# Eight split slots in the raw slots' memory, stage seams by tile and column half, high and low parts from PSUM

## What is computed

```python
shift, scale, gate = _modulation(c, ada_w[i], ada_b[i])      # silu(c) @ ada_w: 1024 x 3072 weights per layer
hx = _rmsnorm(x, norm_g[i]) * (1.0 + scale) + shift
yx = mixer(hx @ w_in, ...) @ w_out
x = x + gate * yx
```

```python
x = x + 0.5 * (silu(h @ w_gate) * (h @ w_up)) @ w_down       # h = rms_norm(x, g); 1024 x 2816, 2816 x 1024
x = x + merged(branches(rms_norm(x, g) @ w_in)) @ w_out      # w_in: 1024 x 7680
x = x + 0.5 * swiglu(...)                                    # a second one, with weights of its own
```

## Time and profile before

| | |
|---|---|
| median of 3 runs | 2111.28 us (2109.96 to 2117.03) |
| the profiled execution's own time | 2106.92 us |
| its span in the trace | 2105.0 us |
| mean granted TensorE clock | 0.978 |
| TensorE busy | 1981.6 us, 94% of the span |
| GpSimd busy | 1381.6 us, 66% |
| ACT, DVE busy | 922.1 us, 639.4 us |
| bytes moved by DMA | 363.97 MB, 173 GB/s over the span |

### The profile page before, as it was taken

One profiled execution on the slowest core, in us unless ns is written; L12 is line 12 of the kernel. 1 busy time (PEld: TensorE's weight loads), 2 busy tenths in 40 slices (PEclk: granted clock), 3 DMA queues, 4 the chain that ended last, 5 costly groups with the idle time before them and its releaser, 6 DMA issues.

```text
span 2105.0 us, 28773 instructions
## 1 busy us (share of the span) xinstructions
PE 1981.6 (94%) x10610; PEld 1684.7 (80%) x10610; DVE 639.4 (30%) x1076; ACT 922.1 (44%) x1324; POOL 1381.6 (66%) x648
## 2 busy tenths in 40 slices
PE   6898989998997989999999999999999999999999
PEld 3667767887675779977888889988988778888987
DVE  4203431455236140035552230013013654133011
ACT  3123321564343454445555454445444554545443
POOL 1331333544674749876857878877887765887886
PEclk9999999999998989999999999999999999999999
DMA  9860276432963527665645547755675554555662
GB/s 330 276 237 24 58 275 231 126 91 82 323 236 100 183 76 199 167 247 150 185 121 166 190 120 192 210 164 141 190 231 180 148 165 126 178 167 151 186 205 91
DMA packets 212216, 363.97 MB, mean 173 GB/s; under 512 B 33508, under 2 KB 106964, under 8 KB 211540
## 3 DMA queue, kind: packets, MB, share of 16 engines
q1 hardware_dynamic: 208656, 351.73, 53.7%
q10 hardware_dynamic: 3460, 10.88, 1.6%
HBM read 361.50 MB, written 6.10 MB: 175 GB/s over the span
## 4 chain that ended last, share of the span: by engine, by line
PE 67%; POOL 8%; issue 8%; DVE 4%; ACT 2%; SPq 1%; DMA 1%; POOLq 0%; ACTq 0%; DVEq 0%
PE ps L949 18%; PE ps L951 18%; PE ps L950 18%; POOL w_lo L461 8%; PE ps L1165 2%; PE ps L1490 1%; PE ps L967 1%; PE ps L1279 1%; PE ps L1531 1%; PE ps L1529 1%; PE ps L1530 1%; DVE xt_lo L1677 1%; DMA raw<-in_ffn_w_down 1%; PE ps L1457 1%; SPq L381 1%
## 5 line engine op out<-in xcount | busy, mean ns | idle before, releaser
L461 POOL TENSOR_TENSOR w_lo<-raw,w_hi 128x1024 fp32r<-128x1024 f32 (+1 forms) x636 | 1362.8, 2154 | 670.0 <-ACT w_hi L507 669.5
L507 ACT ACTIVATE w_hi<-raw 128x1024 fp32r<-128x1024 f32 (+1 forms) x636 | 602.6, 951 | 929.1 <-PE ps L951 856.6
L949 PE MATMUL ps<-w_hi,xt_hi 128*128 128x512 f32 (+2 forms) x2464 | 918.9, 373 | 60.4 <-DVE x_res L1752 16.9
L951 PE MATMUL ps<-w_hi,xt_lo 128*128 128x512 f32 (+2 forms) x2464 | 897.5, 364 | 0.0
L950 PE MATMUL ps<-w_lo,xt_hi 128*128 128x512 f32 (+2 forms) x2464 | 896.3, 364 | 0.0
L949 PEld LDWEIGHTS ps<-w_hi,xt_hi 128*128 128x128 f32 x2464 | 468.6, 190 | 145.8 <-issue 39.8
L951 PEld LDWEIGHTS ps<-w_hi,xt_lo 128*128 128x128 f32 x2464 | 468.7, 190 | 59.4
L950 PEld LDWEIGHTS ps<-w_lo,xt_hi 128*128 128x128 f32 x2464 | 471.0, 191 | 50.8
L1932 DVE TENSOR_TENSOR proj<-proj,ps 128x704 f32 x32 | 28.4, 888 | 446.6 <-PE ps L951 446.6
L1937 DVE TENSOR_TENSOR xt_lo<-ps,xt_hi 128x512 fp32r<-128x512 f32 x44 | 30.0, 690 | 178.6 <-ACT xt_hi L752 178.6
L1165 PE MATMUL ps<-ident,proj 128*128 128x128 f32 x480 | 67.7, 278 | 15.4 <-DVE proj L1917 9.3
(11 more groups left out here) (192 smaller groups left out, 1517.3 us busy)
## 6 DMA issues: line engine op xcount, KB each, us to landing
raw<-in_w_in SPq DMA_DIRECT2D x120, 512.0 KB, 3.7
raw<-in_ffn_w_gate SPq DMA_DIRECT2D x128, 352.0 KB, 3.2
raw<-in_ffn_w_up SPq DMA_DIRECT2D x128, 352.0 KB, 3.4
raw<-in_ffn_w_down SPq DMA_DIRECT2D x88, 512.0 KB, 4.0
pt<-in_ada_w SPq DMA_DIRECT2D x44, 512.0 KB, 4.8
raw<-in_pool_w_in SPq DMA_DIRECT2D x32, 512.0 KB, 4.7
raw<-in_na_w_in SPq DMA_DIRECT2D x32, 512.0 KB, 7.2
raw<-in_conv_w_in SPq DMA_DIRECT2D x32, 512.0 KB, 4.9
```

Of the source, the lines that this page charges most:

```text
L461: pool.tensor_tensor(w_lo[:, s, 0:size], raw[:, g % RAW_SLOTS, 0:size], w_hi[:, s, 0:size].bitcast(F32), ALU.subtract).then_inc(lo_done, 1)
L507: act.activation(w_hi[:, s % SPLIT_SLOTS, 0:SIZES[g]], raw[:, g % RAW_SLOTS, 0:SIZES[g]], ACT.Copy).then_inc(hi_done, 1)
L949: pe.matmul(o, h, hi, start=start, stop=False)
L951: return pe.matmul(o, c, hi, start=False, stop=stop)
```

## The change

**Slots.** There are 8 split slots instead of 4, and they cost no more memory: the low parts lie in the raw slots' own memory (`w_lo` is a second name for `raw`), so GpSimd writes each low part over the values it is made from. SP therefore waits, ahead of each load, for TensorE's use of the group eight before (`group_used`) instead of its low part (`lo_done`). ACT waits for the load alone. GpSimd begins only when the first gains have been made. Where the ada blocks stand in SP's order is not changed; `ADA_AT` and `ADA_LEAD` stay as they are. Within na_out, the loads of NA's bias tables stand earlier in SP's queue (not shown).

```diff
-RAW_SLOTS = 8
-SPLIT_SLOTS = 4
+SLOTS = 8
...
-        raw = sb("raw", [P, RAW_SLOTS, SLOT])
-        w_hi = sb("w_hi", [P, SPLIT_SLOTS, SLOT], F32R)
-        w_lo = sb("w_lo", [P, SPLIT_SLOTS, SLOT], F32R)
+        raw = sb("raw", [P, SLOTS, SLOT])
+        w_hi = sb("w_hi", [P, SLOTS, SLOT], F32R)
+        w_lo = nc.alloc_sbuf_tensor_at("w_lo", [P, SLOTS, SLOT], F32R, offset=nc.lookup_mloc(raw).addr)
...
+        def sum_made(engine, stage, t, nb):
+            if t == 1 and nb == 1:
+                engine.wait_ge(group_used, end_of(stage) + 1)
+            else:
+                engine.wait_ge(pe_done, pe_s.count(("sum", stage, t, nb)))
+        def x_made(engine, stage, t, nb):
+            if t == 1:
+                engine.wait_ge(acc_free[(B0[stage] + nb) % 2], reads(B0[stage] + nb))
+            else:
+                engine.wait_ge(dve_done, dve_s.count(("x", stage, t, nb)))
         def head_rope(m, half=None):
...
-                slot, prev = g % RAW_SLOTS, g - RAW_SLOTS
+                slot, prev = g % SLOTS, g - SLOTS
                 if prev >= 0:
-                    sp.wait_ge(lo_done, on(prev + 1, 8, i))
+                    sp.wait_ge(group_used, on(prev + 1, 8, i))
                 dst = free(raw[:, slot, 0:1], dst_shape)
...
-                s = g % SPLIT_SLOTS
-                pool.tensor_tensor(w_lo[:, s, 0:size], raw[:, g % RAW_SLOTS, 0:size], w_hi[:, s, 0:size].bitcast(F32),
+                s = g % SLOTS
+                pool.tensor_tensor(w_lo[:, s, 0:size], raw[:, s, 0:size], w_hi[:, s, 0:size].bitcast(F32),
...
+            pool.wait_ge(dve_done, dve_s.count(("first_gains", 0, 1)))
...
-                    act.wait_ge(raw_in[g % RAW_SLOTS], on(16 * (g // RAW_SLOTS + 1), 16, i))
-                    if s >= SPLIT_SLOTS:
-                        act.wait_ge(group_used, on(g - SPLIT_SLOTS + 1, 8, i))
-                    act.activation(w_hi[:, s % SPLIT_SLOTS, 0:SIZES[g]], raw[:, g % RAW_SLOTS, 0:SIZES[g]],
+                    act.wait_ge(raw_in[g % SLOTS], on(16 * (g // SLOTS + 1), 16, i))
+                    act.activation(w_hi[:, g % SLOTS, 0:SIZES[g]], raw[:, g % SLOTS, 0:SIZES[g]],
                                    ACT.Copy).then_inc(hi_done, 1)
```

```diff
+            def rms_halves(key, prev, t):
+                for nb in range(2):
+                    x_made(act, prev, t, nb)
+                    act.activation(free(proj[:, 0:1], [[1, 512]], t * D + nb * 512), stream(t)[:, nb * 512:(nb + 1) * 512], ACT.Square,
+                                   accum_out=stat[:, 2 * t + nb:2 * t + nb + 1]).then_inc(act_done, act_s.one(("ss", key, t, nb)))
+                act.wait_ge(act_done, act_s.count(("ss", key, t, 1)))
+                act.wait_ge(dve_done, dve_s.count(("ssb", key, t)))
+                act.activation(rstat[:, t:t + 1], stat[:, 2 * t + 1:2 * t + 2], ACT.Sqrt, bias=stat[:, 8 + t:9 + t],
+                               scale=1.0 / D).then_inc(act_done, act_s.one(("rms", key, t)))
...
-                                   free(full[:, 0:1], [[P, n], [1, P]], (t % 2) * 1024 + u * n * P),
+                                   ps[:, turn_bank(key, t, u), 0:n * P].rearrange("p (c n) -> p c n", c=n),
...
+            def high_of_normed(key, t, prev, gain):
+                for u in range(4):
+                    act.wait_ge(pe_done, pe_s.count(("tp", key, t, u)))
+                    tile_free(prev, t)
+                    for f in (2 * u, 2 * u + 1):
+                        last = act.activation(xt_hi[0][:, f, t * P:(t + 1) * P], ps[:, turn_bank(key, t, u), (f % 2) * P:(f % 2 + 1) * P],
+                                              ACT.Copy, scale=cols[:, gain + f:gain + f + 1])
+                    last.then_inc(act_done, act_s.one(("xhi", key, t, u)))
...
+            def after_half(key, prev, k, gain):
                 load_sqrt(k)
-                act.wait_ge(dve_done, dve_s.count(("x", prev, 0)))
-                rms(key, 0, stream(0))
                 split(3)
-                high_of_tile(key, 0, prev, half=0)
+                rms_halves(key, prev, 0)
                 split(1)
-                for b in (B0[prev], B0[prev] + 1):
-                    act.wait_ge(acc_free[b % 2], reads(b))
-                rms(key, 1, stream(1))
-                high_of_tile(key, 0, prev, half=1)
-                high_of_tile(key, 1, prev)
+                high_of_normed(key, 0, prev, gain)
+                rms_halves(key, prev, 1)
+                high_of_normed(key, 1, prev, gain)
```

```diff
+                    x_made(pe, prev, t, 0)
...
+                turn_at = k0 + (1 if stage[0] in "fm" else 2)
                 for t in tiles:
-                    for k in range(k0, k1):
-                        s = (g + k) % SPLIT_SLOTS
-                        if then and t == tiles[-1] and k == k1 - 1:
-                            if len(tiles) > 2:
-                                pe.wait_ge(dve_done, dve_s.count(("sums_read", stage, 3)))
-                            turn_tile(then, 0)
-                        if t == tiles[0]:
-                            pe.wait_ge(lo_done, g + k + 1)
-                            if k % 2 == 0:
-                                for st in range(len(tiles) // 2):
-                                    pe.wait_ge(dve_done, dve_s.count(("xt", key, st, k // 2)))
-                        for nb in range(2):
+                    for nb in range(2):
+                        for k in range(k0, k1):
+                            s = (g + k) % SLOTS
+                            if then and t == tiles[-1] and nb == 1 and k == turn_at:
+                                if len(tiles) > 2:
...
+                                turn_tile(then, 0)
...
                             last = mm3(ps[:, bank_of(b + nb, t), :], t, place(k), w_hi[:, s, nb * 512:(nb + 1) * 512],
                                        w_lo[:, s, nb * 512:(nb + 1) * 512], False, k == k1 - 1)
-                        if t == tiles[-1]:
-                            last.then_inc(group_used, 1)
-                        elif k == k1 - 1:
-                            last.then_inc(pe_done, pe_s.one(("sum", stage, t)))
+                            if t == tiles[-1] and nb == 1:
+                                last.then_inc(group_used, 1)
```

```diff
+            def sum_of_squares(key, t):
+                dve.wait_ge(act_done, act_s.count(("ss", key, t, 0)))
+                dve.tensor_scalar(stat[:, 8 + t:9 + t], stat[:, 2 * t:2 * t + 1], 1.0 / D, EPS, ALU.mult,
+                                  ALU.add).then_inc(dve_done, dve_s.one(("ssb", key, t)))
...
+                        v = ps[:, turn_bank(key, t, u), (f % n) * P:(f % n + 1) * P]
+                        last = dve.tensor_scalar(v, v, scale(t // 2, f), shift(t // 2, f), ALU.mult, ALU.add)
...
+            def low_of_normed(key, t, gain):
+                for u in range(4):
+                    dve.wait_ge(act_done, act_s.count(("xhi", key, t, u)))
+                    for f in (2 * u, 2 * u + 1):
+                        last = dve.scalar_tensor_tensor(
+                            out=xt_lo[0][:, f, t * P:(t + 1) * P], in0=ps[:, turn_bank(key, t, u), (f % 2) * P:(f % 2 + 1) * P],
+                            scalar=cols[:, gain + f:gain + f + 1], in1=xt_hi[0][:, f, t * P:(t + 1) * P].bitcast(F32),
+                            op0=ALU.mult, op1=ALU.subtract)
+                    last.then_inc(dve_done, dve_s.one(("xt", key, t, u)))
...
+            def gated_sum(stage, key, t, nb):
...
+                sum_made(dve, stage, t, nb)
+                if t in (0, 2) and nb == 0:
+                    dve.wait_ge(act_done, act_s.count(("gate", key, t // 2, 1)))
+                v = ps[:, bank_of(B0[stage] + nb, t), :]
+                o = (t // 2) * 1024 + nb * 512
+                dve.tensor_tensor(v, v, pt[:, o:o + 512], ALU.mult).then_inc(dve_done, dve_s.one(("gated", stage, t, nb)))
+                dve.wait_ge(dve_done, dve_s.count(("gated", stage, t, nb)))
+                r = stream(t)[:, nb * 512:(nb + 1) * 512]
+                last = dve.tensor_tensor(r, v, r, ALU.add)
                 if t == 1:
-                    dve.wait_ge(group_used, end_of(stage) + 1)
+                    last.then_inc(acc_free[(B0[stage] + nb) % 2], 1)
...
+            def half_sum(stage, t, nb, factor):
+                sum_made(dve, stage, t, nb)
+                r = x_res[:, t, nb * 512:(nb + 1) * 512]
+                last = dve.scalar_tensor_tensor(out=r, in0=ps[:, bank_of(B0[stage] + nb, t), :], scalar=factor, in1=r, op0=ALU.mult,
+                                                op1=ALU.add)
+                if t == 1:
+                    last.then_inc(acc_free[(B0[stage] + nb) % 2], 1)
...
+            def after_half(key, prev, factor, gain):
+                half_sum(prev, 0, 0, factor)
+                half_sum(prev, 0, 1, factor)
+                sum_of_squares(key, 0)
+                x_made(dve, prev, 0, 1)
                 normed(key, 0)
-                scaled_tile(key, 0, *how, half=0)
```

(9 more changed lines are left out.)

229 lines of the change are left out of this document (106 added, 123 removed).

## The result

| | before | after |
|---|---|---|
| median of the runs | 2110.62 us (4 runs, 2106.70 to 2117.03) | 2158.90 us (4 runs, 2158.43 to 2159.31) |
| span of the profiled execution | 2105.0 us | 2156.6 us |
| mean granted clock | 0.978 | 0.975 |

The changed kernel is slower: the ratio is 1.0226, with a 95% interval of 1.0200 to 1.0251. The forecast was 2149 us in a range of 2106 to 2182.

The account below looks back on a forecast made before the run. TensorE was taken as the bound, so only its waits could be won. Gains of 35 us against losses of 73 made 38 us slower than the profiled 2106.9, 2145, or 2149 us for the median, range 2106 to 2182.

Parts of the forecast that it names:

- The loss by the slots: Slots refilled only after TensorE's use delay ada blocks and w_down behind them in SP's queue: 73 us lost (43 to 99).
- cv_in: Six ada blocks in cv_in each come 5.0 us late, plus clock: 34 us lost (24 to 42).
- na_in: Seven of eight ada blocks in na_in each cost 2.3 us and 1 of clock: 17 us lost.
- p0_in: Ada blocks 4 to 6 late, block 4 behind ACT's table loads, less 5.5 us saved by earlier splits: 16 us lost.
- f1_down: w_down lands later, behind small tables and a load TensorE must release: 6 us lost for both layers.
- The gains: Shorter TensorE waits at half and gated seams, context tiles and f10: 35 us won (15 to 48).
- Half seams: Five seams before mix_in, f2_in and f1_in1: waits for x_res shrink, 20 us won (8 to 26).
- Gated seams: Three seams before na_in, cv_in and p3_in: each wins 3 us with clock, 9 us (3 to 14).
- Context and f10: Context tiles' 6.0 us of waits halve, 3 us; the seam before f10 wins the contention alone, 3 us.
- Rival 2: Seams win little: L1652 waits a whole GpSimd instruction and the turn stops TensorE; gains 12, 2172 us, chance 0.12.
- rival 3: Loads drain faster and stalls are half the forecast's, seams win in full: 2112 us, no change, chance 0.08.

Follow-up runs that it names:

- lead4: The changed kernel with ADA_LEAD 4 instead of 6, so each ada block is sent two loads earlier: 2075.02 us, ratio 0.9855.
- late_ada: The kernel before, with SP waiting ahead of each ada block for TensorE's use of the group two before the block's own: 2167.63 us, ratio 1.0292.
- slots_only: The kernel before with only the slots changed and NA's bias tables in the new order: 2204.92 us, ratio 1.0471.
- act_norm: The changed kernel with ADA_LEAD 4 and tables moved, plus half and gated seams' normed rows by ACT, not DVE: 2051.76 us, against 2052.40 without the latter.
- norm_first: lead4 with the next stage's first four splits behind tile 0's squares in half and gated seams: 2079.78 us, ratio 0.9859.
- no_gains_wait: lead4 without GpSimd's wait for the first gains: 2078.12 us, ratio 0.9856.

## Why the prediction was right, and where its terms were off

**The loss by the slots: foreseen 73 us, measured 94 to 99.** Its mechanism was right in each place: the block stands behind a load that TensorE must release, the lead is one group, and both lead4 and late_ada show it from their side.
- *cv_in, "34 us (24 to 42)":* 38.0, in the bounds (34.7 in slots_only). From TensorE's last use of group at - 2 to the end of a block's products it is a sum of three terms, and each was a little short. The first quarter was issued 0.6 us later ("0.5"), the last landed 9.1 to 11.1 us after that, 9.8 in the mean ("9.2"), and the last products took 1.0 to 1.9 us ("0.5"). The "5 for the clock" came out in size, 4.9 us over the "0.5", but only 2.2 of it is the clock's. late_ada lost 25.2 us in this stage with the products at 1.00.
- *na_in, "17 us (10 to 24)":* 24.5, just over the bound (26.8 in slots_only). The term that was short is the landing time. The 7.9 us taken were those of a block with no load ahead of it; behind the load of group at + 6 it was 8.9 to 9.8, some 10 us over the seven blocks, and the last products took 1.0 and not 0.5, some 4 us more.
- *p0_in, "16 us (6 to 24)":* 23.2 (20.6 in slots_only). The text had block 4 done "at 86"; it was done at 92.9. "Until about 82 us" for the tables was too early, since the last of them landed at 86.4 (85.2 in the kernel before). The two loads ahead landed at 77.9 and 85.6, and the four quarters, put at "80 to 86", from 87.3 to 91.3.
- *f1_down, "6 us (3 to 9)":* the wait grew by 5.6 us in layer 0 alone, 10 us for both. The failed term is the slack. w_down was sent 5.2 us ahead of the start of TensorE's last matmul in f1_in, where it was 10.1 before: 4.9 us later, as foreseen. Its first load took 9.1 us and not 8.5. But the text let TensorE start 3.5 us after the landing and so had 2.4 us left over; it starts 6.18 us after it, before and after, since ACT's high part of the rows stands behind four splits of w_down. So the whole delay came through.

**The gains: foreseen 35 us, measured 42 to 52.**
- *Half seams, "20 us":* the time across the five, measured as for act_norm above, was 24.2 us shorter. The two before mix_in, where L1693 meets GpSimd, won 3.2 and 4.3, the others 5.1 to 5.8, where it met nobody. The text took 0.8 us for that meeting at each of five, 4.0 in all; by act_norm it costs 1.7 us at two, 3.5 in all.
- *Gated seams, "9":* 14.4 (5.3, 3.6 and 5.5). The middle one, before cv_in, is the one where L1693 met GpSimd. They were left with waits of 1.3 to 1.5 us for a turn, where the text had "2.9 us of 5.2 stay".
- *Context and f10, "3" and "3":* the context tiles' wait fell from 6.0 to 4.2, 1.8 us; the seam before f10 is 5.0 us shorter.
- *Not in the sum:* 3.3 us at the start, by GpSimd's wait for the first gains, which the text didn't price.

The net was 48 us and not 38: the loss was 21 to 26 us larger and the gain 7 to 17 us. That the total came so near is in part luck, since the two errors had opposite signs. Rival 2's mechanism (L1652 waits a whole GpSimd instruction) came true at two half seams and one gated seam, at 1.7 us each, and the gains stayed far above its 12 us; rival 3 (loads drain faster) was wrong by its sign, since blocks took longer to land.

The rule cited in the prediction, from the Trainium skill (SBUF — State Buffer, "SBUF: two separate sides" and "Who interferes with whom"), holds here for L1693, for which no row of before told: 0.75 us with GpSimd idle, 2.88 when it starts inside an instruction of GpSimd's, 0.76 again in norm_first. Operations with an operand in PSUM do not show it (L1728: 343 ns alone, 345 beside GpSimd). DVE operations with two inputs in SBUF do, down to 8 columns (no_gains_wait above).

For the two queues of p0_in the Trainium skill (DMA: Bandwidth & Descriptors, "Queues, rings and completion order") says that each transfer engine goes round the queues it has work for, one packet each. The trace agrees by its packet records: 338 of ACT's queue and 300 of SP's between 62 and 76 us, and 492 and 491 between 67 and 82 us in lead4. The turns are nearly even and the packets are not, 9.3 KB in the mean against 2.0 KB, so ACT's queue moved 3.15 MB and SP's 0.59. Whether tables in smaller packets would have held the block up less was not tried.

What stays open: of the 13 us by which late_ada's cv_in is shorter than the changed kernel's, 11 are shorter landing times of the six blocks and 2 the clock. That loads in flight make the landing longer is argued from these times alone; no kernel here took those loads away and left the rest. Why a late quarter's products start in pairs stays open too.

## What to carry to other kernels

When a buffer is freed by a later event than before, don't ask only whether its own next load is in time: look at everything that stands behind that load in the same queue, and count its lead anew. Here one number, the place of the large loads in the queue, decided between 2.3% slower and 1.4% faster. Don't put a long stretch at a low granted clock down to the clock before you have set the start of each operation beside the landing of its operand: here a late block took 5.8 us at 0.50 and 4.9 at 1.00, since its data came in pieces. And follow a wait to the engine that stands in front of it in program order: f1_down's first product waited for DVE, DVE for ACT, and ACT for a load that has nothing to do with those rows. A change of two independent halves is worth running as halves: the gain of some 45 us was there all the time, under a loss of twice that.

## What was not expected of the hardware

- A block of 2 MB needs 7.8 us by itself (269 GB/s), 9.1 to 11.1 with one to three loads of 512 KB under way, and 29.8 beside transfers from DRAM to DRAM of another queue, all from the first quarter's issue to the last one's landing.
- After 4.9 us of standing still the next 5.8 us of matmuls ran at a granted clock of 0.50, and the clock was at 1.00 in the window from 584 us on. It cost 0.9 us there and 2.2 in all of cv_in. In late_ada TensorE stood still for 1.1 to 1.5 us in front of each of the six blocks of cv_in, and their products ran at 1.00.
- DVE's operation on one tensor in SBUF took 2.88 us behind GpSimd and 0.75 alone, and GpSimd's next instruction then 2.84 and not 2.4; ACT's for the same rows took 1.15 us in either case. Two DVE operations of 4 columns took 2.33 us together beside GpSimd and 0.23 without it.
